# Prompt attention by pairs of key groups: scores and values as two tiles side by side, probabilities weighed and then turned, and a weight ring that runs across layers

## What is computed

```python
def win_attend(q, kv, q_pos, k_pos, slopes):
    s = jnp.einsum('bqtgrd,bqsgd->bqtgrs', q, kv[:, :, :, 0])
    ...
    s = s - slopes * dist
    p = masked_softmax(s, mask)
    return jnp.einsum('bqtgrs,bqsgd->bqtgrd', p, kv[:, :, :, 1])
...
    ga = jax.nn.sigmoid(gate_a).reshape(B, T, 3, G, R)
    o_a = (ga[:, :, 0, :, :, None] * o_cmp + ga[:, :, 1, :, :, None] * o_slc
           + ga[:, :, 2, :, :, None] * o_win)
...
    mix = jax.nn.sigmoid(g_ma) * (o_a @ w_pa) + jax.nn.sigmoid(g_mb) * (o_b @ w_pb)
```

## Time and profile before

| | us |
|---|---|
| median of 3 runs | 2889.31 |
| lowest and highest | 2883.48, 2893.99 |
| the profiled execution, device time | 2889.56 |
| its span, first to last instruction | 2887.8 |
| TensorE busy in it | 2633.5 (91%) |
| DVE busy | 793.8 (27%) |
| ACT busy | 523.7 (18%) |
| mean granted TensorE clock | 0.939 of full |

### The profile page before, as it was taken

How to read it: one execution, slowest core, us unless ns; L and a number is a source line. 1 busy time by engine, 2 the same in 40 slices (tenths; PEclk the granted TensorE clock), 3 DMA queues, 4 the chain that set the end, 5 groups by cost and what they waited for, 6 DMA issues and landing times.

```text
span 2887.8 us, 31540 instructions
## 1 busy us (share of the span) xinstructions
PE 2633.5 (91%) x13454; PEld 2130.7 (74%) x13454; DVE 793.8 (27%) x1817; ACT 523.7 (18%) x991; POOL 95.1 (3%) x172
## 2 busy tenths in 40 slices
PE   7998789997899899999979887899978989999998
PEld 6776567775788788888857755677767878888887
DVE  2344322335311222110014443223343122212101
ACT  1143111233100111100012431013321011111100
POOL 2010000000000000000000100000000000000000
PEclk9998898998799999999989988999988999999999
DMA  7144421100122122212161534211011211222122
GB/s 237 39 173 157 161 74 44 27 19 30 32 73 76 44 73 73 73 46 82 54 202 57 187 125 160 74 44 30 15 32 44 76 59 59 73 73 73 53 71 70
DMA packets 184514, 228.52 MB, mean 79 GB/s; under 512 B 37438, under 2 KB 170868, under 8 KB 180020
## 3 DMA queue, kind: packets, MB, share of 16 engines
q1 hardware_dynamic: 173944, 133.08, 15.5%
q0 software_dynamic: 10432, 93.44, 8.5%
HBM read 218.15 MB, written 16.66 MB: 81 GB/s over the span
## 4 chain that ended last, share of the span: by engine, by line
PE 83%; DVE 7%; ACT 4%; DMA 3%; issue 2%; POOL 1%; DVEq 0%; SPq 0%; POOLq 0%; ACTq 0%
PE PS L756 45%; PE PS L1246 11%; PE PS L778 6%; ACT arena L1277 4%; PE PS L845 4%; PE PS L1077 3%; PE PS L410 2%; DVE arena L1527 2%; PE PS L833 2%; DVE arena L1518 2%; DMA arena<-in_state_kv_win_dram 1%; PE PS L1091 1%; PE PS L952 1%; DMA ring<-in_w_in_dram 1%; PE PS L809 1%
## 5 line engine op out<-in xcount | busy, mean ns | idle before, releaser
L756 PE MATMUL PS<-hT,ring 128*128 128x272 f32 (+1 forms) x4672 | 1105.2, 399 | 30.6 <-DMA ring<-in_w_in_dram 19.1
L756 PEld LDWEIGHTS PS<-hT,ring 128*128 128x128 f32 (+1 forms) x4672 | 894.6, 192 | 238.9 <-issue 27.0
L1277 ACT ACTIVATE arena<-PS 64x512 f32<-64x512 f32 (+15 forms) x426 | 237.8, 570 | 1389.8 <-PE PS L756 740.4
L1246 PE MATMUL PS<-arena,ring 128*128 128x272 f32 x1408 | 323.5, 393 | 1.9 <-DVEq L2071 1.9
L1246 PEld LDWEIGHTS PS<-arena,ring 128*128 128x128 f32 x1408 | 267.2, 190 | 57.6 <-DVEq L2071 2.7
L1527 DVE COPY arena<-PS 64x512 f32<-64x512 f32 (+6 forms) x213 | 154.3, 725 | 368.8 <-PE PS L756 171.7
L1518 DVE TENSOR_TENSOR arena<-PS,arena 128x544 f32<-128x544 f32 (+3 forms) x120 | 73.0, 620 | 500.1 <-PE PS L756 423.6
L778 PE MATMUL PS<-ring,hT 128*128 128x256 f32 (+1 forms) x800 | 181.6, 388 | 0.0
L756 PE MATMUL PS<-arena,ring 128*128 128x272 f32 x768 | 177.2, 393 | 3.2 <-DVE arena L1518 3.2
L756 PEld LDWEIGHTS PS<-arena,ring 128*128 128x128 f32 x768 | 145.8, 190 | 33.9 <-DVE arena L1518 4.0
L1524 DVE SCALAR_TENSOR_TENSOR arena<-arena,prm 128x32 f32<-128x32 f32 (+2 forms) x178 | 90.5, 509 | 291.8 <-ACT arena L1277 288.7
(11 more groups left out here) (262 smaller groups left out, 1757.2 us busy)
## 6 DMA issues: line engine op xcount, KB each, us to landing
ring<-in_w_up_dram SPq DMA_DIRECT2D x88, 512.0 KB, 4.2
ring<-in_w_in_dram SPq DMA_DIRECT2D x68, 512.0 KB, 4.7
ring<-in_w_down_dram SPq DMA_DIRECT2D x32, 384.0 KB, 3.4
ring<-in_w_down_dram SPq DMA_DIRECT2D x32, 320.0 KB, 4.0
arena<-in_state_kv_win_dram POOLq DMA_DIRECT2D x4, 2048.0 KB, 8.2
ring<-in_w_out_dram SPq DMA_DIRECT2D x16, 512.0 KB, 4.6
out_dram<-in_state_kv_win_dram POOLq DMA_DIRECT2D x2, 4064.0 KB, 23.0
ring<-in_w_in_dram SPq DMA_DIRECT2D x16, 256.0 KB
```

The costliest lines, as they stand in the source:

```text
L756: mm = pe.matmul(PS[0:m, b + a, 0:HALF], weight(k), rhs(k)[:, HALF * a:HALF * a + HALF], start=(k == 0), stop=(k == nk - 1))
L1246: mm = pe.matmul(PS[:, b + a, 0:HALF], w[:, k, :], aT[:, 11 * half + k, HALF * a:HALF * a + HALF], start=(half == 0 and k == 0), stop=(hal ...
L1277: return nc.scalar.activation(out, in_, func, **kw)
```

## The change

The unit becomes (query tile, r, br): one branch of the two heads r and 4 + r, one of each key group g. There are still 32 units a layer.

- `score(j)`: the two products use partitions 0 to 63 and 64 to 127 of `qT` and `kT`, so different rows of the array. The same is done in the block scores, by swapping the loops over g and r.
- `weigh(j)` on DVE takes the place of `combine(j)`: after the exponentials, reciprocal and gate as before, and then two multiplications of `ex` by that weight (128 by w each). It signals `pn`, and TensorE now waits for `pn` ahead of its transposes and not for ACT's `ep`. `ex` gets three buffers.
- The transposes go one bank per group, from a new pool E (banks 0 to 2), and ACT copies each group apart.
- `values(j)`: 64 columns of values are stationary, 128 columns of transposed probabilities move, and the two groups write partitions 0 to 63 and 64 to 127 of one bank (`VBANK`, bank 3). All units of a query tile and the blocks' values add up in that bank; DVE copies it once per tile to `AT` (`attended`). `A`, the block products `po` and the 16 transposes at the end are gone; `block_values` does two products of 512 columns per tile inside the loop.
- The blocks' probabilities are weighed on DVE ahead of their transposes as well (one more operation of 128 by 248).
- The side work of the units claims pool S.
- The first load of each slot in a layer waits for the last use of that slot in the layer before: `q0` for `d6`, `q1` and `kv0` for `d7`.

```diff
-            return S.at(eng, f"filled_{S.ticket(eng, 'd7')[0]}", 0)
+            last = [x for i, x in enumerate(WSTEPS) if i % WSLOTS == s][-1]
+            return S.filled_before(eng, last_ticket(last))
...
-            for br in range(2):
-                for t in range(qt + 1):
-                    mm = pe.matmul(PS[:, b + br, 0:HD], PTp[j % 2][:, br, P * t:P * t + P], kv[:, t, 1 + br, P + HD * g:P + HD * g + HD],
-                                   start=(t == 0), stop=(t == qt))
+            for t in range(qt + 1):
+                for g in range(G):
+                    mm = pe.matmul(PS[HD * g:HD * g + HD, VBANK, P * r:P * r + P], kv[:, t, 1 + br, P + HD * g:P + HD * g + HD],
+                                   PTp[j % 2][:, g, P * t:P * t + P], start=False, stop=(r == R - 1 and br == 1 and t == qt))
...
-                    for br in range(2):
-                        mm = pe.matmul(PS[:, b + br, 0:P * (qt + 1)], qT[HD * g:HD * g + HD, r, P * qt:P * qt + P],
+                    for g in range(G):
+                        mm = pe.matmul(PS[:, b + g, 0:P * (qt + 1)], qT[HD * g:HD * g + HD, r, P * qt:P * qt + P],
                                        kT[HD * g:HD * g + HD, br, 0:P * (qt + 1)], start=True, stop=True)
...
+                def block_values(qt):
+
+                    if qt:
+                        pe.wait_ge(*S.at(pe, "at_out", qt))
+                    for g in range(G):
+                        pe.matmul(PS[HD * g:HD * g + HD, VBANK, :], vcp[0:NBLK_P, HD * g:HD * g + HD], PcT[0:NBLK_P, qt, R * g:R * g + R, :],
+                                  start=True, stop=False)
...
-                    pe.wait_ge(*S.at(pe, "ep", j + 1))
-                    pe.wait_ge(*S.claim(pe, "T", f"e{qt}{h}"))
+                    side(("u", j), "S")
+                    pe.wait_ge(*S.at(pe, "pn", j + 1))
+                    for g in range(G):
+                        pe.wait_ge(*S.claim(pe, "E", f"e{j}{g}"))
...
-                pe.wait_ge(*S.at(pe, "a_ready", 1))
-                for qt in range(QT):
-                    pe.wait_ge(*S.claim(pe, "T", f"at{qt}"))
...
+                def weigh(j):
...
                     dv.wait_ge(*S.at(dv, "ep", j + 1))
...
+                    for g in range(G):
+                        last = tsc(ex[j % 3][:, g, 0:w], ex[j % 3][:, g, 0:w], small[:, c0 + 6 + g:c0 + 7 + g], ALU.mult)
+                    last.then_inc(*S.inc(dv, "pn"))
+
+                def attended(qt):
+
+                    dv.wait_ge(*S.at(dv, "pv", 2 * R * (qt + 1)))
+                    copy(AT[:, :, P * qt:P * qt + P], PS[:, VBANK, :].rearrange("p (r n) -> p r n", r=R)).then_inc(*S.inc(dv, "at_out"))
 
                 maxima(0)
                 for j in range(len(units)):
                     if j + 1 < len(units):
                         maxima(j + 1)
+                    weigh(j)
                     side_copy(("u", j))
-                    if j:
-                        combine(j - 1)
+                    if j >= 2 and (j - 2) % (2 * R) == 2 * R - 1:
+                        attended((j - 2) // (2 * R))
```

More of the change, by code:

```diff
@@ L119, in claim @@
         self.tickets[(pool, phase, l)] = n + 1
-        where, use = pool + str(n % 2), n // 2
+        where, use = pool + str(n % POOLS[pool][1]), n // POOLS[pool][1]
         assert l or (name, phase) not in self.tickets, name
@@ L127, in banks @@
         where = self.ticket(eng, name)[0]
-        return {"T": 0, "S": 4}[where[0]] + 2 * int(where[1])
+        first, _, width = POOLS[where[0]]
+        return first + width * int(where[1])
     def fill(self, eng, name):
@@ L137, in filled, with filled_before @@
         return self.at(eng, f"filled_{where}", use + 1)
+    def filled_before(self, eng, name):
+        where, use = self.ticket(eng, name)
+        phase, l = self.part[eng]
+        if l == 0:
+            return self.at(eng, f"filled_{where}", 0)
+        self.part[eng] = (phase, l - 1)
+        back = self.filled(eng, name)
+        self.part[eng] = (phase, l)
+        return back
     def drain(self, eng, name):
@@ L310, in build @@
         vcp = sb("vcp", P)
[L311 to L318, removed]
+        ex = [carve(1024 * i, 2, SEQ) for i in range(3)]
+        PTp = [carve(3072 + 1024 * i, 2, SEQ) for i in range(2)]
+        PcT = carve(5120, QT, HEADS, P)
+        zp = carve(9216, HEADS, NBLK_P)
+        zpm = carve(9472, HEADS, NBLK_P)
         rT = carve(10048, GH, NT)
@@ L1062, in _ @@
                     side(("c", qt, 1))
[L1063 to L1069, removed]
@@ L1071, in score @@
-                def score(j):
[L1072 to L1075, removed]
-                    for br in range(2):
-                        mm = pe.matmul(PS[:, b + br, 0:P * (qt + 1)], qT[HD * g:HD * g + HD, r, P * qt:P * qt + P],
-                                       kT[HD * g:HD * g + HD, br, 0:P * (qt + 1)], start=True, stop=True)
-                    mm.then_inc(*S.fill(pe, f"s{qt}{h}"))
+                units = [(qt, r, br) for qt in range(QT) for r in range(R) for br in range(2)]
@@ L1094, in _ @@
                         values(pe, units, j - 1)
                 values(pe, units, len(units) - 1)
-                pe.wait_ge(*S.at(pe, "a_ready", 1))
-                for qt in range(QT):
-                    pe.wait_ge(*S.claim(pe, "T", f"at{qt}"))
-                    b = S.banks(pe, f"at{qt}")
-                    for r in range(R):
-                        mm = pe.transpose(PS[:, b, P * r:P * r + P], A[:, qt, r, :, :], ident[:, :])
-                    mm.then_inc(*S.fill(pe, f"at{qt}"))
+                for g in range(G):
+                    pe.wait_ge(*S.drained(pe, f"e{len(units) - 1}{g}"))
@@ L1881, in combine @@
-                def combine(j):
-                    qt, h = units[j]
-                    g, r = h // 4, h % 4
+                    if j >= 3:
+                        dv.wait_ge(*S.filled(dv, f"e{j - 3}1"))
+                    dv.wait_ge(*S.filled(dv, f"s{j}"))
+                    b = S.banks(dv, f"s{j}")
+                    dv.nop().then_inc(*S.inc(dv, "settled"))
+                    for g in range(G):
+                        last = nc.vector.tensor_tensor_reduce(ex[j % 3][:, g, 0:w], PS[:, b + g, 0:w], dtab[:, 384 - P * qt:512], 1.0, -3e38, ALU.add, ALU.max, small[:, c0 + g:c0 + g + 1])
```

114 lines of the change are left out of this document (49 added, 65 removed).

## The result

| | us |
|---|---|
| before, median beside the runs of after | 2887.18 |
| after, median of 4 | 2969.28 |
| ratio after / before | 1.0276, 95% interval 1.0252 to 1.0300 |
| change measured | +82 |
| change forecast | +35 (2925, range 2880 to 2972) |

The changed kernel is slower, as forecast, and its time lies in the range, but the loss is more than twice the one that the sum gave.

The account below looks back on a forecast made before the run. It took TensorE, busy 91% of the span, to bound the kernel. Per layer 8.8 (loop) + 22.6 (clock) - 6.1 (block branch), twice, less 15.4 once (ring), made +35.2 us: 2925 us, 1.2% slower, range 2880 to 2972.

Parts of the forecast that it names:

- Products side by side: Unit loop: score and value products run in pairs on different rows or columns, 17 us less per layer on each.
- The rival without pairs: Unit loop: pairs do not run together, 34 us more per layer, 2994 us; chance 0.03.
- The wait that comes in: Unit loop: TensorE waits for DVE's `pn`; units without side work become serial, 2.9 to 6.0 us for k = 1 to 4.
- the loop overlaps after all: Unit loop: TensorE alone needs 129 us per layer, 2760 us in all; chance 0.05.
- The loop at full clock: Unit loop at 2.4 GHz: 188.6 us per layer, 8.8 us more than the 179.8 before.
- The clock: Unit loop: waits throw TensorE to half clock for part of the work, 22.6 us per layer, bounds 0 and 51.
- the first stretch before: First 33 us of the old loop, granted clock 0.69; source of the 0.6 half-clock share for k = 1, 2.
- the bound of 51: Unit loop: all units without side work and their side works' starts at half clock, 51 us per layer.
- The block branch: Block branch: `po` goes and scores pair, while DVE's weighing adds 0.84 us of waiting per tile; -6.1 us per layer.
- At most 3 us worse if the longer pauses cost clock: Block branch: limit on what lower clock could take from its -6.1 us per layer.
- The ring: Turn of the layer: `q0` loads earlier, so TensorE's wait shrinks by 14.0 and products by 1.4; -15.4 us once.
- The rival with the low clock in all units: Unit loop: clock low in all units without side work, 2982 us; chance 0.12.

Follow-up runs that it names:

- experiment 5: Changed kernel with weigh(j) ahead of the next maxima on DVE: 2842.65 us one unit ahead, 2801.1 us with scores and maxima two units ahead.
- the waits filled: Changed kernel with 4 + 2k unread products of 128 columns in TensorE's waits, in units without side work: 2887.69 us, ratio 0.9992.
- experiment 4: Changed kernel with unread products in TensorE's waits of units without side work: 2962.55 us with 8 + 4k of them, 2887.69 us with 4 + 2k.
- the ring alone: Kernel before the change with only the new wait of the weight ring: 2874.66 us beside 2891.29 of before, ratio 0.9946.
- these waits filled: Kernel with weigh(j) first and two units ahead, plus 9 or 11 unread products ahead of each block branch wait: 2794.1 us, ratio 0.9672.
- the first try: Changed kernel with 8 + 4k unread products of 128 columns in TensorE's waits of units without side work: 2962.55 us, ratio 1.0250.

## Why the prediction was right in kind and wrong in size

**Products side by side: right.** A score of 512 columns takes 1.13 us (forecast 1.11, before 1.98), 16 value records 1.09. The rival without pairs falls.

**The wait that comes in: right, step by step.** At k = 4: from the score to DVE's start 1.32 us (forecast 1.11 + 0.18), maxima to the reciprocal 684.49 - 683.07 = 1.42 (1.42), reciprocal to the last product of the weighing 684.88 + 0.88 - 684.49 = 1.27 (1.26), to TensorE 0.06. The multiplication that before did not show costs 0.48 us for two at k = 1 and 0.88 at k = 4, so my nearest row was the right one. The rival "the loop overlaps after all" needed another order on DVE, as said; with it (experiment 5) the loop takes 147 to 150 us, not the 129 of TensorE's bare sum; 8.8 us of the difference are idle time, and the rest is not divided.

**The loop at full clock: 2.4 us short.** Forecast 188.6, measured 191.0 and 191.3 with the waits filled. Some 1.1 us of it are the eight units with side work (76.1 us from transposes to transposes for a forecast of 75; 10.54 for 10.35 at k = 4), and a part of the rest is the fill itself (6.12 for 6.06 us at k = 4), so the clock term below is measured a little too small, if anything.

**The clock: the step that failed.** The term was 22.6 us per layer, with bounds of 0 and 51. Measured: 229.7 - 191.0 = 38.7 and 232.2 - 191.3 = 40.9. The groups of layer 1's loop, first of the changed kernel, then with the waits filled (count, then busy us and mean ns), divide it:

```profile
L767 PE MATMUL PS<-hT,ring 128*128 128x272 f32 x256 | 65.8, 418 | 0.0
L1081 PE MATMUL PS<-kv_kT,qT 64*128 64x128 f32 (+3 forms) x128 | 35.4, 643 | 0.6 <-issue 0.6
L420 PE MATMUL PS<-arena,kv_kT 128*64 128x128 f32 x320 | 35.2, 371 | 0.0
L1105 PE MATMUL PS<-ident,arena 128*128 128x128 f32 x160 | 33.7, 360 | 57.2 <-DVE arena L1529 57.2
L1090 PE MATMUL PS<-arena,vcp 31*64 31x512 f32 x16 | 7.9, 1082 | 0.0
```

```profile
L767 PE MATMUL PS<-hT,ring 128*128 128x272 f32 x256 | 60.8, 396 | 0.0
L1081 PE MATMUL PS<-kv_kT,qT 64*128 64x128 f32 (+3 forms) x128 | 25.6, 480 | 0.6 <-issue 0.6
L420 PE MATMUL PS<-arena,kv_kT 128*64 128x128 f32 x320 | 24.4, 283 | 0.0
L1111 PE MATMUL PS<-ident,arena 128*128 128x128 f32 x160 | 24.0, 281 | 4.3 <-DVE arena L1535 3.2
L1090 PE MATMUL PS<-arena,vcp 31*64 31x512 f32 x16 | 4.3, 613 | 0.0
```

Side work lost 5.0 us (6 forecast: right). Scores, values and transposes lost 9.8 + 10.8 + 9.7 = 30.3, where I had 16.6, and `block_values` lost 3.6, which I had not put under the clock at all. By query tile the windows of experiment 4 give 7.6, 9.2, 8.2 and 13.7 us lost for k = 1 to 4, where my shares made 3.8, 6.2, 5.6 and 7.0. The wrong step is the share of the small products that I put at half clock (30.3 of 39 us went, 0.78): 0.6 for k = 1, 2, taken from the first stretch before, and 0.35 above "where the work before each pause is longer". But the pause grows with k as well, from 1.74 to 2.94 us, and at k = 4 TensorE is still idle for 49% of a pitch of 6.06. The stretch of before that I borrowed the 0.6 from was busy for 92%, and I had put it beside a loop idle half of the time; the low stretch in my own rows (busy for 47%, clock 0.50) was the nearer one and pointed at the bound. My reason for the low clock in that first stretch was also misread: of the products before, only the scores use half of the array, while the values had a 128*128 tile standing in it.

The Trainium skill (TensorE: Matmul & The Clock Gate, HAM oscillation) tells of a kernel that waits for DMAs between its bursts and starts each next one cold, "Every single K-tile." The trace here, with shorter waits for DVE of 1.74 to 2.94 us, agrees in direction (in layer 1, behind 18 of 24 such waits the transposes are at half clock wholly or in part) but not in full: a clock thrown back behind every wait would have cost the bound of 51, where 30.3 + 5.0 = 35.3 us went.

**The block branch: right at full clock, then eaten by it.** The wait ahead of the transposes grew from 1.46 to 2.35 us, +0.89 for a forecast of +0.84; pairs of block scores take 1.08, 0.47 less than the 1.55 before (0.6 forecast). Layer 1 gained 6.3 us (6.1 forecast), layer 2 only 1.1. The match in layer 1 is luck: in the kernel before, the same instructions took 98.92 us in layer 1 and 93.00 in layer 2, at a granted clock of 0.90 and 0.96 (the number behind POOL's), so 5.9 us more stood in layer 1 by the clock alone. With the ring alone, which leaves this branch as it was, they took 105.3 and 93.0 us.

```profile
397.25:496.17 98.92, 92.09 (x449) 73.62 (x448) 19.63 (x47) 5.69 (x8) 5.84 (x8) 0.90 0.15 44
1832.82:1925.82 93.00, 86.17 (x449) 70.55 (x449) 19.63 (x47) 5.69 (x8) 5.82 (x8) 0.96 0.15 47
```

"At most 3 us worse if the longer pauses cost clock" was the right mechanism and too small a bound: with these waits filled the branch takes 5 us less, and its 87.8 us in layer 2 are 5.2 less than the 93.0 before.

**The ring: right in its wait, in part luck in its sum.** 19.10 to 5.30 us of idle time is -13.8 (-14.0 forecast), and the chip gave 16 us for the ring alone. The further 1.4 us from a faster start of the products did not come in the changed kernel (32.57 us, not 31.18; with the ring alone it is 31.00). The stretch as a whole gave 17.3 in place of 15.4, and 17.0 with the ring alone. Of that, 3.1 us came further on in a row of 80 records of 24 columns that the change leaves alone: it took 12.58 us before (from 1557.60, granted clock 0.60) and 9.50 after (from 1584.54, 0.81).

Against the sum: clock +34.4 for both layers, loop at full clock +5.1, block branch +4.8, ring -1.9, untouched stages -2.7; together 39.7 above +35.2, the 74.8 of the traces. The rival with the low clock in all units, 2982 us, was the closest of all to 2969, and I had given it only 0.12.

## What to carry to other kernels

When an edit puts a wait on TensorE into every round of a loop, price it twice: the wait itself, and all the work around it at half clock. Where TensorE would be idle for half of each round, the upper bound of the clock term is the better guess, not a middle: here 30.3 of 39 us of the small products went. This is one kernel, and rounds of 3 to 6 us.

A chain over engines is cut by the order in which the waited-for engine takes its own work, not by how far ahead the loop looks: two units ahead alone gave 4 us, one exchange of two calls on DVE gave 122 us, both together 164.

To learn what the clock costs in a stage, fill its waits with unread products that fit inside them. Size them by a trace of that very product: the first try was twice too long and hid a gain of 77 us all but completely (2 us).

## What was unexpected of the hardware

- Adding 54.6 us of unread work per layer made the changed kernel 77 us faster. Its loop in layer 1 went from a granted clock of 0.77 to 1.00.
- A product of two full 128 x 128 fp32 tiles costs twice the transposition of the same size: 24 unread records (12 products) took 2.94 us, 0.24 per product, and 8 transposes 1.04, 0.13 each. I had priced the product like the transposition.
- The half clock comes and goes inside a round: at 685.82 the transposes and values were at half, at 689.48 the score that followed them at full (1.13 us), at 697.35 the next score at half again (2.08).
